# mLSTM scan: log weights as fp32r products, exponential from PSUM, 64-row tiles, division on POOL

## What is computed

```
b = jnp.cumsum(lf, axis=-1)
d = jnp.where(tril, b[..., :, None] - b[..., None, :] + li[..., None, :], -jnp.inf)
m_t = jnp.maximum(b + m[..., None], jnp.max(d, axis=-1))
w = jnp.exp(d - m_t[..., None])
g_inter = jnp.exp(b + m[..., None] - m_t)
s = jnp.einsum('bhtd,bhsd->bhts', q, k) * w
num = jnp.einsum('bhts,bhsv->bhtv', s, v) + g_inter[..., None] * jnp.einsum('bhvd,bhtd->bhtv', cmat, q)
nq = jnp.sum(s, axis=-1) + g_inter * jnp.einsum('bhd,bhtd->bht', nvec, q)
h = num / jnp.maximum(jnp.abs(nq), jnp.exp(-m_t))[..., None]
cmat = decay[..., None, None] * cmat + jnp.einsum('bhs,bhsv,bhsd->bhvd', w_end, v, k)
```

## Time and profile before

| | us |
|---|---|
| median of three runs | 2967.2 |
| lowest, highest | 2962.0, 2974.21 |
| the profiled execution | 2986.19 |
| its span | 2984.5 |
| TensorE matmuls busy | 2379.0 (80%) |
| VectorE busy | 2015.0 (68%) |
| ScalarE busy | 1213.4 (41%) |
| POOL busy | 408.1 (14%) |

### The profile page before, as it was taken

How to read it: one execution, slowest core, us unless ns; L and a number is a source line. 1 busy time by engine, 2 the same in 40 slices (tenths; PEclk the granted TensorE clock), 3 DMA queues, 4 the chain that set the end, 5 groups by cost and what they waited for, 6 DMA issues and landing times. The chain is left out here.

```text
span 2984.5 us, 40907 instructions
## 1 busy us (share of the span) xinstructions
PE 2379.0 (80%) x15564; PEld 1998.9 (67%) x15564; DVE 2015.0 (68%) x3841; ACT 1213.4 (41%) x2272; POOL 408.1 (14%) x366
## 2 busy tenths in 40 slices
PE   4877886786979759898968787967768787698888
PEld 0667775665868649777817576856667676597777
DVE  0477866788967665575715778577889766656766
ACT  2443243333746435443224422433338563454421
POOL 0002003322000120011200020042220001100212
PEclk9988897898979869899979888988979989799999
DMA  8200010000000100001371000100000000000022
...
DMA packets 21049, 112.61 MB, mean 38 GB/s; under 512 B 2464, under 2 KB 2464, under 8 KB 15776
## 3 DMA queue, kind: packets, MB, share of 16 engines
...
...
## 5 line engine op out<-in xcount | busy, mean ns | idle before, releaser
L1699 DVE TENSOR_REDUCE a_st<-ps 128x1 f32<-128x1280 f32 (+1 forms) x160 | 203.6, 1274 | 24.1 <-PE ps L1611 23.2
L1670 ACT ACTIVATE ring<-ps,a_st 128x1280 f32<-128x1280 f32 (+1 forms) x160 | 184.8, 1155 | 76.8 <-DVE a_st L1699 76.4
L1945 PE MATMUL ps<-g_x_hi,g_w_hi 128*128 128x512 f32 (+1 forms) x480 | 176.7, 368 | 32.1 <-DVE g_gate L1984 15.4
L1946 PE MATMUL ps<-g_x_lo,g_w_hi 128*128 128x512 f32 (+1 forms) x480 | 175.6, 366 | 0.0
L1947 PE MATMUL ps<-g_x_hi,g_w_lo 128*128 128x512 f32 (+1 forms) x480 | 173.3, 361 | 0.0
L426 PE MATMUL ps<-a_proj_wh,a_proj_xh 128*128 128x512 f32 (+1 forms) x320 | 118.1, 369 | 65.7 <-DVE a_proj_xl L407 65.5
L1967 ACT ACTIVATE g_x_hi<-hT 128x1280 fp32r<-128x1280 f32 x80 | 101.4, 1272 | 143.6 <-PE ps L1947 141.5
L1611 PE MATMUL ps<-a_k,a_q 128*128 128x512 f32 (+1 forms) x416 | 131.0, 420 | 25.9 <-ACT ring L1670 21.3
L241 PE MATMUL ps<-ring,csil 128*2 128x512 f32 x192 | 93.9, 646 | 71.6 <-DMA ring<-in_w 70.7
L2064 PE MATMUL ps<-o_w_hi,o_y_hi 128*128 128x512 f32 x320 | 127.1, 397 | 16.4 <-ACT o_y_hi L2120 16.4
L2000 DVE TENSOR_TENSOR g_x_lo<-hT,g_x_hi 128x1280 fp32r<-128x1280 f32 x80 | 119.1, 1489 | 29.9 <-ACT g_x_hi L1967 29.9
...
## 6 DMA issues: line engine op xcount, KB each, us to landing
...
```

The costliest lines, as they stand in the source:

```text
L1670: act.activation(p(u, c, n), ps[:, 3 * c:3 * c + 3, :].rearrange("p b n -> p (b n)")[:, 0:n], ACT.Exp, bias=st[:, 0:1], accum_out=st[:, 1: ...
L1699: dve.tensor_reduce(stat[:, u % SLOTS, c, 0:1], ps[:, 3 * c:3 * c + 3, :].rearrange("p b n -> p (b n)")[:, 0:n], AX.X, ALU.max, negate=Tru ...
L1945: pe.matmul(out, w_hi[:, at, cols], x_hi[:, at, toks], start=k == 0, stop=False)
L1946: pe.matmul(out, w_hi[:, at, cols], x_lo[:, at, toks], start=False, stop=False)
```

## The change

q is kept once, over all 128 partitions, and POOL's part of the projection block goes. In the scan, copies in fp32r of the mask, of an identity, of the selection matrix and of the rows (a high and a low part, in two halves of the partitions) are made at the block's start. The log products add the mask in PSUM, through the identity; ScalarE reads PSUM and adds the key's column as its bias, head by head, into a double buffer. Scores and inter part use 64 rows of TensorE for each head, with `tile_position` 0 or 64, and different PSUM banks for even and odd heads; scores have one buffer and come behind the fresh states and the inter part. The division goes from VectorE to POOL, between the scalings of v, and `num` and `den` are double buffers. The diff, cut:

```diff
-q_of = [yT[:, 6 + h // 2, :] if h % 2 else qkT[:, h // 2, :] for h in range(HEADS)]
...
-        pool.wait_ge(silu_ready.sem, 2)
-        pool.memset(yT[0:64, 6:8, :], 0.0).then_inc(q_cleared.sem, 1)
-        pool.wait_ge(q_cleared.sem, 1)
-        for c in range(2):
-            pool.wait_ge(act_s.sem, 3 + c)
-            pool.tensor_tensor(yT[64:P, 6 + c, :], qkT[64:P, c, :], conv_in[64:P, c, :], ALU.mult).then_inc(q_moved.sem, 1)
-            pool.wait_ge(q_moved.sem, c + 1)
-            pool.memset(qkT[64:P, c, :], 0.0).then_inc(q_cleared.sem, 1)
-            pool.wait_ge(q_cleared.sem, c + 2)
...
-        pe.wait_ge(q_moved.sem, 2)
...
-            dve.tensor_tensor(qkT[0:64, c, :], qkT[0:64, c, :], conv_in[0:64, c, :], ALU.mult).then_inc(silu_ready.sem, 1)
+            dve.tensor_tensor(qkT[:, c, :], qkT[:, c, :], conv_in[:, c, :], ALU.mult).then_inc(silu_ready.sem, 1)
...
+    row_parts = tile("b_row_parts", [P, T], F32R)
+    sel = tile("b_sel", [P, 8, P], F32R)
+    neg = tile("b_neg", [P, 2, P], F32R)
+    same = tile("b_same", [P, P], F32R)
+    wgt = tile("b_wgt", [P, 2, HEADS, P])
     sw = tile("b_sw", [P, HEADS, P])
...
+    num = tile("b_num", [P, 2, HEADS, DH + 1])
+    den = tile("b_den", [P, 2, HEADS])
...
+    def fresh_of(u, hp=slice(0, 2)):
+        return ps[:, 4 + 2 * (u % 2), 2 * (DH + 1):4 * (DH + 1)].rearrange("p (a d) -> p a d", a=2)[:, hp, :]
+
+    def intra_of(u):
+        return ps[:, 5 + 2 * (u % 2), 2 * (DH + 1):6 * (DH + 1)].rearrange("p (h d) -> p h d", h=HEADS)
+
+    def inter_of(u):
+        return ps[:, 4 + 2 * (u % 2):6 + 2 * (u % 2), 0:2 * (DH + 1)].rearrange("p o (e d) -> p e o d", e=2)
...
-        for u, (way, i, j) in enumerate(UNITS):
+        pool.tensor_copy(neg[:, :, :], C(env, "neg").rearrange("p (a b) -> p a b", a=2)).then_inc(parts.sem, 1)
+        pool.tensor_copy(same[:, :], C(env, "ident")).then_inc(parts.sem, 1)
+
+        def scale_v(u):
+            way, i, j = UNITS[u]
             if u >= 2:
                 pool.wait_ge(u_mm.sem, u - 1)
             pool.tensor_tensor(vw[:, u % 2, :, :], v1[:, j, :, :],
                                col(j, 3, way).unsqueeze(2).broadcast_to([P, HEADS, DH + 1]), ALU.mult)\
                 .then_inc(vw_ready.sem, 1)
+        def divide(u):
+            way, i, j = UNITS[u]
+            rec = den[:, u % 2, :].unsqueeze(2).broadcast_to([P, HEADS, DH])
+            n = num[:, u % 2, :, 0:DH]
+            pool.wait_ge(rec_ready.sem, u + 1)
+            if second_visit(u):
+                pool.tensor_tensor(n, n, rec, ALU.mult).then_inc(divided.sem, 1)
+                pool.wait_ge(divided.sem, 2 * u + 1)
+                pool.tensor_tensor(hB[:, j, :, :], hB[:, j, :, :], n, ALU.add).then_inc(divided.sem, 1)
+            else:
+                pool.tensor_tensor(hB[:, j, :, :], n, rec, ALU.mult).then_inc(divided.sem, 2)
+
+        scale_v(0)
+        scale_v(1)
+        for u in range(NU):
+            divide(u)
+            if u + 2 < NU:
+                scale_v(u + 2)
+        pool.wait_ge(divided.sem, 2 * NU)
+
...
+            if u == 0:
+                pe.wait_ge(parts.sem, 2)
+                pe.wait_ge(lows.sem, 3)
             if u >= 2:
-                pe.wait_ge(dm_ready.sem, HEADS * (u - 1))
+                pe.wait_ge(w_ready.sem, HEADS * (u - 1))
+            bank = ps[:, u % 2, :]
+            pe.matmul(bank.rearrange("p (h t) -> p h t", h=HEADS), same[:, :],
+                      neg[:, way, :].unsqueeze(1).broadcast_to([P, HEADS, P]), start=True, stop=False, skip_group_check=True)
             for h in range(HEADS):
-                last = pe.matmul(ps[:, u % 2, h * P:(h + 1) * P], sel[:, way * HEADS + h, :],
-                                 yT[:, 3, j * P:(j + 1) * P], start=True, stop=True)
+                last = pe.matmul(bank[:, h * P:(h + 1) * P], sel[:, way * HEADS + h, :], row_parts[:, span(u)],
+                                 start=False, stop=h == HEADS - 1, skip_group_check=True)
...
-            j = UNITS[u][2]
-            t0, t1 = j * P, (j + 1) * P
-            if u >= 2:
-                pe.wait_ge(sw_ready.sem, u - 1)
+            if u >= 1:
+                pe.wait_ge(sw_ready.sem, u)
             for h in range(HEADS):
-                last = pe.matmul(ps[:, 2 + u % 2, h * P:(h + 1) * P], qkT[:, 2 + h // 2, t0:t1], q_of[h][:, t0:t1],
-                                 start=True, stop=True)
+                last = pe.matmul(ps[:, 2 + h % 2, h // 2 * P:(h // 2 + 1) * P], qkT[half(h), 2 + h // 2, span(u)],
+                                 qkT[half(h), h // 2, span(u)], start=True, stop=True, tile_position=(64 * (h % 2), 0))
             last.then_inc(s_mm.sem, 1)
...
-            t0, t1 = j * P, (j + 1) * P
             if u + 1 < NU:
                 logs(u + 1)
-                scores(u + 1)
...
-                pe.wait_ge(finished.sem, u - 1)
-            for h in range(HEADS):
-                pe.matmul(ps[:, 5 + 2 * (u % 2), h * (DH + 1):(h + 1) * (DH + 1)], q_of[h][:, t0:t1],
-                          state[:, way, h // 2, :], start=True, stop=True)
+                pe.wait_ge(state_ready.sem, 2 * (u - 1))
+                pe.wait_ge(num_ready.sem, u - 1)
             pe.wait_ge(vw_ready.sem, u + 1)
             for h in range(HEADS):
-                r = slice(64 * (h % 2), 64 * (h % 2) + 64)
-                a = (HEADS + h // 2) * (DH + 1)
-                last = pe.matmul(ps[r, 5 + 2 * (u % 2), a:a + DH + 1], ktm[:, j, h * DH:(h + 1) * DH],
+                last = pe.matmul(fresh_of(u)[half(h), h // 2, :], ktm[:, j, h * DH:(h + 1) * DH],
                                  vw[:, u % 2, h, :], start=True, stop=True)
+            for h in range(HEADS):
+                last = pe.matmul(inter_of(u)[:, h // 2, h % 2, :], qkT[half(h), h // 2, span(u)],
+                                 state[half(h), way, h // 2, :], start=True, stop=True, tile_position=(64 * (h % 2), 0))
             last.then_inc(u_mm.sem, 1)
+            if u + 1 < NU:
+                scores(u + 1)
             pe.wait_ge(sw_ready.sem, u + 1)
             for h in range(HEADS):
-                last = pe.matmul(ps[:, 4 + 2 * (u % 2), h * (DH + 1):(h + 1) * (DH + 1)], sw[:, h, :], v1[:, j, h, :],
-                                 start=True, stop=True)
+                last = pe.matmul(intra_of(u)[:, h, :], sw[:, h, :], v1[:, j, h, :], start=True, stop=True)
             last.then_inc(intra_mm.sem, 1)
...
-        for u in range(NU):
-            act.wait_ge(dm_ready.sem, HEADS * (u + 1))
-            if u >= 1:
-                act.wait_ge(sw_ready.sem, u)
-            act.activation(wgt[:, :, :], logw[:, :, :], ACT.Exp).then_inc(w_ready.sem, 1)
+        for u, (way, i, j) in enumerate(UNITS):
+            act.wait_ge(d_mm.sem, u + 1)
+            if u >= 2:
+                act.wait_ge(sw_ready.sem, u - 1)
+            for h in range(HEADS):
+                act.activation(wgt[:, u % 2, h, :], ps[:, u % 2, h * P:(h + 1) * P], ACT.Exp, bias=col(j, 0, way)[:, h:h + 1])\
+                   .then_inc(w_ready.sem, 1)
...
+        dve.tensor_copy(row_parts[0:64, :], yT[0:64, 3, :]).then_inc(lows.sem, 1)
+        dve.tensor_copy(sel[:, :, :], C(env, "sel_row").rearrange("p (a b) -> p a b", a=8)).then_inc(lows.sem, 1)
         dve.memset(state[:, :, :, :], 0.0).then_inc(zeroed.sem, 1)
+        dve.wait_ge(lows.sem, 1)
+        dve.tensor_tensor(row_parts[64:P, :], yT[0:64, 3, :], row_parts[0:64, :].bitcast(F32), ALU.subtract)\
+           .then_inc(lows.sem, 1)
...
-            if second_visit(u):
-                dv2.link(dve, dve.tensor_tensor(num[:, :, 0:DH], num[:, :, 0:DH], rec, ALU.mult))
-                dv2.link(dve, dve.tensor_tensor(hB[:, j, :, :], hB[:, j, :, :], num[:, :, 0:DH], ALU.add))
-            else:
-                dv2.link(dve, dve.tensor_tensor(hB[:, j, :, :], num[:, :, 0:DH], rec, ALU.mult))
-            dve.wait_ge(dv2.sem, dv2.n)
-            dve.sem_inc(finished.sem, 1)
...
-        def log_weights(u):
-            way, i, j = UNITS[u]
-            dve.wait_ge(d_mm.sem, u + 1)
-            if u >= 1:
-                dve.wait_ge(w_ready.sem, u)
-            for h in range(HEADS):
-                dve.scalar_tensor_tensor(out=logw[:, h, :], in0=ps[:, u % 2, h * P:(h + 1) * P],
-                                         scalar=col(j, 0, way)[:, h:h + 1], in1=neg[:, way, :],
-                                         op0=ALU.add, op1=ALU.min).then_inc(dm_ready.sem, 1)
...
+        def weigh(u):
+            dve.wait_ge(w_ready.sem, HEADS * (u + 1))
             dve.wait_ge(s_mm.sem, u + 1)
             if u >= 1:
                 dve.wait_ge(intra_mm.sem, u)
-            dve.tensor_tensor(sw[:, :, :], ps[:, 2 + u % 2, :].rearrange("p (h t) -> p h t", h=HEADS), wgt[:, :, :],
-                              ALU.mult).then_inc(sw_ready.sem, 1)
-            if u >= 1:
-                finish(u - 1)
-        finish(NU - 1)
+            for o in range(2):
```

(32 more changed lines are left out.)

50 lines of the change are left out of this document (11 added, 39 removed).

## The result

The changed kernel takes 3028.7 us (median of four runs, 3024.46 to 3031.97) where the kernel before, on the same chip, takes 2970.67 (four runs, 2962.0 to 2974.21). The ratio is 1.0202, 95% interval 1.019 to 1.0215: slower by 58 us. The prediction was 2932 us, range 2913 to 2957. It was wrong, in sign too. Its rival "The clock stays low (slower)", with 3030 us and a chance of 0.06, is what came.

What follows compares the result with a forecast made beforehand. VectorE and TensorE were both taken as near their limit in the scan. Per layer 79.3 us against 93.5 gains 14.2, plus 3.2 before it makes 17.4; two layers 34.8, so 2932 us, range 2913 to 2957.

Steps and rivals of the forecast that it cites:

- The clock stays low (slower): Rival: TensorE at 1.2 GHz for the whole scan, 6 us per unit, 3030 us in all; chance 0.06.
- the clock's: Scan start: the 4 us pause loses the full clock, one unit at half clock, 2.5 us per layer, bounds 0 and 5.
- TensorE's own unit: Scan: TensorE's work per unit, logs 0.77, scores and inter 1.10, fresh states 0.43, intra 0.95, together 3.25 us.
- First visits: Scan units visiting a token tile for the first time: period 3.3 us, half of the two-unit loop.
- second visits: Scan units visiting a token tile again, with one POOL operation more: period 3.65 us.
- The loop through POOL over two units: Scan: v's scaling for u+1 queues behind the division of u-1, so weighting u to u+2 takes 6.63 us.
- Start of the block: Scan start: the first log product waits for the copies, 4.0 us new per layer, between 3.3 and 5.5.
- Projection block: Before the scan: without POOL's work the convolution ends earlier, gain 3.2 us per layer, bounds 2.5 and 3.8.
- Tiles don't pay: Rival: 64-row products in the scan run one at a time, TensorE 4.15 us per unit, 2958 us; chance 0.07.
- POOL and VectorE block each other: Rival: in the scan VectorE's denominator waits up to 0.62 us for POOL, 12.4 us a layer, 2957 us; chance 0.05.
- fp32r products cost 0.22: Rival: 128-column fp32r products cost as today's, TensorE 3.7 us per unit, 16 us of gain lost, 2948; chance 0.07.
- The tail: Scan end: intra part, finish and division of the last unit, 4.3 us per layer.

Runs made afterwards that it cites:

- warm start: The changed kernel with eight fp32 products of 512 columns ahead of each layer's first log product: 2949.9 us.
- early copies: The changed kernel with its fp32r copies made in the projection block instead of at the scan's start: 2933.0 us; four later executions 2927.2 to 3031.66.

## Why the prediction was wrong, point by point

**The step that failed** is the clock's: "The new 4 us pause at the start will lose the full clock. At half clock a unit takes TensorE about 5.9, so one unit there costs 2.5 us. Bounds 0 and 5." That the scan starts low was right, and so was the unit at half clock (5.82). The cause was not: in the profiled execution the clock was lost in the convolution, and the transposes didn't bring it back; the run with fp32 log products shows the way that was meant. What failed in the sum is the silent step behind it, that one unit of work brings the clock back, as it does in the kernel before. Not one of the 40 units got it back. In place of 2.5 us per layer it was 19 periods of 2.4 us more each, 45 us (110.8 against 65.6).

**The rival came true, but not by its evidence.** Its price of 3030 us came within 2 us of the median, with a unit of 6 us put at 5.82 by the trace. Against it stood "at half clock TensorE would have none", that is no pauses. That came true, 111.00 of 111 us busy, and was no argument: a busy TensorE isn't enough. For it stood the GLA scan's 10 us at 0.50 with TensorE busy for 9.0 of 10. But that scan came back. This is how the same trace of the kernel before goes on:

```profile
490.00:500.00 10.00, 9.33 (x154) 8.20 (x152) 8.02 (x16) 2.82 (x3) 3.90 (x4) 1.00 0.01 2
```

It stays at 1.00 up to 560. Its first tiled products start at 478.79, so with small tiles and fp32r products it took 11 us of scan to get back. Read to its end, the row would have put the slow start at some 11 us, which is two units of 5.9 and 5 us of loss, the prediction's own upper bound, and not at the whole scan. None of the rows shows a mix that stays low. That 3030 was on the list was good; that it came so close was luck.

The Trainium skill ("TensorE: Matmul & The Clock Gate", Part 1) has the clock follow from how busy TensorE has been. By that rule the changed scan would be at full clock within its first units; the traces here differ, and they decide.

**What held,** as seen where the clock is high: TensorE's own unit 3.25 (measured 3.19); scores and inter part as tiles 1.10 (1.09, from 273.09 to 274.18); mask and log products 0.77 (0.80, from 271.90 to 272.70). First visits 3.3 (3.31, the mean of 3.19 and 3.43), second visits 3.65 (3.66, the mean of 3.19 and 4.12), and so 19 periods 65.9 (65.6). Not so VectorE: it was to be idle for about a fifth of the scan and is for over a third (busy for 41.93 of 65.00 us with the warm start). The loop through POOL over two units was right in cause and size.

**Start of the block** 4.0, bounds 3.3 and 5.5: 3.7 us, from 259.66 to 263.37, TensorE without a matmul for 4.60. Inside it POOL was held up beside VectorE: two scalings (L738) took 2.80 us where they take 0.6 each alone. That cost nothing, since the first log product waited for VectorE's subtraction (L828).

**Projection block** 3.2, bounds 2.5 and 3.8: 3.6. L621 takes 0.48 where L633 took 3.01, and the two products (L687) 2.89 for all 128 partitions where L699 took 5.59 for 64. This agrees with the Trainium skill ("SBUF — State Buffer", Who interferes with whom), by which a VectorE instruction that reads two operands from SBUF and a POOL instruction that reads SBUF contend for a read interface that they share.

**The other rivals.** "Tiles don't pay" is out: with full rows a unit takes 3.89, with tiles 3.19. "POOL and VectorE block each other" in the scan: with the warm start the three operations from the denominator to the reciprocal take 0.17, 0.16 and 0.18, as in the kernel before; out. "fp32r products cost 0.22" is out: four take 0.48 us, 0.12 each. (Its price was off too: by the prediction's own numbers TensorE's 3.7 us in 19 periods makes 70.3 against 65.9, 9 us less gain in all and not 16.)

**The tail** was the one other term off: forecast 4.3, measured 6.2 with the warm start (from the last weighting at 336.90 to 343.15), as the last unit runs with little beside it: its fresh states start at 337.38, 0.61 us late behind POOL's scaling, its intra part runs from 338.35 to 339.83, its `finish` from 339.94 to 341.70, and its division is two operations (to 343.15). Put together, start 3.7, fill 2.5 (from the first log product to the first weighting, warm start), periods 65.6 and tail 6.2 are 78.0 us per layer, where the forecast had 76.8 besides its 2.5 for the clock. By this sum the change would have won about what was forecast, had the clock held.

**What stays open.** Which property of the mix decides (columns, rows in use, fp32 or fp32r) is known only as far as the runs on it go: fp32 log products and full-row scores bring the clock back, a full-row inter part and one more fp32r product don't, one more fp32 product did in one layer of two. Nor is it known what decides, from run to run and layer to layer, the clock that the transposes of k leave: much the same transposes brought it back in the kernel before, with fp32 log products and with the early copies, and not in the changed kernel.
